# Gathering and summing the rows of the experts on chip, by matrices of zeros and ones on TensorE, in a two-block transformer kernel

## The chip, the cores and the metric

The kernel runs on one core of a Trainium2 chip (trn2), as one launch. The metric is the device time of one execution in microseconds. Before the change it is 2328.91 us, the median of three runs (2328.08 to 2332.37).

## What is computed

512 tokens of width 1024 in float32 go through two transformer blocks. The first has two kinds of attention and a mixture of experts, then a norm; the second starts with a norm of its own, a retention and a latent attention, then a feed-forward layer.

```
x = x + hybrid_mixer(rms_norm(x, attn_norm), ...)
h = rms_norm(x, ffn_norm)
x = x + hier_moe(h, w_group, b_group, w_expert, b_expert, w1, w3, w2)
x = rms_norm(x, final_norm)          # end of the first block
xn = rmsnorm(x, pre_mix_norm_2)      # start of the second block
...

def hier_moe(h, ...):
    # softmax over 8 groups, the best group; in it the best 2 of 8 experts
    gate = g_w * softmax(top_v)                # two gates per token
    expert_id = g_idx * 8 + top_i              # two of 64 experts per token
    # rows of a token go to its experts
    ys[e] = (silu(xb @ w1[e]) * (xb @ w3[e])) @ w2[e]     # 1024 -> 512 -> 1024
    out[token] += gate * ys                    # a sum of two rows per token
```

There are 1024 assignments (512 tokens, two experts each). The three matrices of one expert hold 6 MiB in float32, those of all 64 experts 384 MiB.

## The kernel before

Every engine has its own program, and semaphores tie them together; nothing is scheduled by a planner, so the order on each engine is the order of the code. SyncE (SP) issues all loads of weights, ScalarE (ACT) small loads, GpSimd (POOL) the indirect DMAs.

**Dense parts.** x (4 tiles of 128 tokens) stays in SBUF. Weights come in units of 8 KiB per partition into `raw` (three slots). ACT copies a unit to `w_hi` (`hi_until`, L622, the copy is L631) and DVE puts the rest into `w_lo` (`lo_until`, L634, the subtraction is L640); both have two slots. PE multiplies in three passes (L562 to L564) and waits for `w_lo` in `loaded`. `order` is the list of all units; those from `n_first` on belong to the second block, and `ahead` asks for the unit behind the one that is in use. `pe_to_feature` (L557) turns tokens into features by transposes; `dve_split_jobs` and `act_split_jobs` (L670, L657) take the result apart.

**Routing.** DVE makes `h2`, the normed rows (L1976), PE transposes it, the router's matmuls (L1780) give 72 logits per token, and `dve_route` (L1091) takes the best group and its two best experts. `onehot` and `both` are 0/1 rows over the 64 experts; PE sums them by `C("before")` and `C("ones")` into the rank of each assignment in its expert. DVE then makes `pos_t`, 512 times the expert plus the rank. Experts are worked in blocks of 32 rows (`BLK`); one with more than 32 assignments would get further blocks, listed behind the first 64, and `blk` holds block, expert and count. In these inputs the loop works 64 blocks.

**From lists to rows.** POOL scatters the assignment ids by `pos_t` into `slot_ids` in HBM (eight indirect DMAs, L2047), reads them back (L2051), DVE casts them (L1189), PE transposes them (L1814), and DVE writes `asg_tab` (L1194) and `tok_tab` (L1197). Then it raises `m_ready`, for which SP, PE, ACT, DVE and POOL wait. `h2` goes to `h_rows` in HBM (L2042).

**The loop over pairs of blocks** (`pe_pair`, `act_pair`, `dve_pair`, `pool_pair`; u is 0 or 1 in a pair, the last pair stands outside the loop). POOL copies a column of the table and gathers a block's rows from `h_rows` to `Xe` (L2060). PE transposes them (`rows_to_columns`, L1825, eight transposes), ACT copies them to `XTs` (L1661). `hidden(u, h)` (L1834) multiplies half of the 1024 features by half of w1 and w3: 16 matmuls, in which four column groups of PE work side by side. DVE copies the result to `Hs` (L1985), PE transposes it (L1862), ACT applies Silu (L1676), DVE multiplies by the other half (`aT`, L1987), and `down(u, h)` (L1843) multiplies by w2, 16 matmuls for both h. ACT copies that to `y_b` (L1680), and POOL scatters it to `y_rows` in HBM (L2065), a row per assignment and quarter.

**The ring.** Weights of experts lie in twelve slots of 1 MiB, six per u: four for w1 and w3, two for w2. SP loads the twelve of the first pair ahead of the routing; in the loop it reloads a slot when `w_used` says that PE has done with it (L1531). PE waits for `landed` of each.

**Behind the loop.** POOL waits for all scatters (`m_done`) and reads `y_rows` back in four DMAs (L2100). DVE adds gate times row, two per token tile (L2001), ACT squares x (L539), the root follows (`dve_rstd`, L544, L548, L550), DVE writes the normed x with the final gain (L2009), ACT squares it again for the second norm, and DVE writes `xn` (L2016), for whose four tiles PE waits in `pe_second` before the transposes hT3. Meanwhile ACT and DVE have split two units of weights, between these steps. `dve_second` (L1200) then begins with the angles of the rotations (`dve_angles`, L855) and asks for further units behind them.

PSUM's banks in the loop: bank 0 for the rows' transposes, 1 for those of the hidden rows, 2 and 3 for the hidden products of u = 0 and 1, 4 and 5 for the down products.

Of the kernel before, what the change touches and what calls it, by code (L numbers as in the profile page):

```python
# [20 lines left out]
F32 = mybir.dt.float32  # L21
# [8 lines left out]
P = 128  # L30
# [36 lines left out]
def constants():  # L67
# [41 lines left out]
    put("id2", np.concatenate([2.0 * (p + P * np.arange(NT)[None, :]) + k for k in range(2)], 1))  # L109
# [14 lines left out]
def route_constants():  # L124


    a = np.zeros((P, 128), np.float32)
# [4 lines left out]
    a[:, 97] = np.arange(P) // BLK  # L132
# [54 lines left out]
def build(nc, a, out):  # L187
    ctx = ExitStack()
    with ctx:
# [47 lines left out]
        y_b = [at(f"y_b{u}", F0 + 5120 + Q * u, [Q]) for u in range(2)]  # L237
        Xe = [at(f"Xe{u}", F0 + 28672 + D * u, [D])[0:BLK, :] for u in range(2)]
# [23 lines left out]
        h_rows = nc.dram_tensor("h_rows", (T, D), F32, kind="Internal").ap()  # L262
        y_rows = nc.dram_tensor("y_rows", (8 * T, Q), F32, kind="Internal").ap()
        c_rows = nc.dram_tensor("c_rows", (H1, T), F32, kind="Internal").ap()
        slot_ids = nc.dram_tensor("slot_ids", (NE * T, 1), I32, kind="Internal").ap()
# [169 lines left out]
        plan("ids", 2)  # L435
# [452 lines left out]
        w_used = sem("w_used")  # L888
        xt_filled, xt_out = sem("xt_filled"), sem("xt_out")
# [3 lines left out]
        gathered, scattered = [sem(f"gathered{u}") for u in range(2)], [sem(f"scattered{u}") for u in range(2)]  # L893
        idx_copied = sem("idx_copied")
        m_done, m_ready = sem("m_done"), sem("m_ready")
        pe_step, pool_step = sem("pe_step"), sem("pool_step")
        XTb, Ab = banks[0], banks[1]
        Hb, Yb = banks[2:4], banks[4:6]
# [3 lines left out]
        tok_tab = scratch[0:BLK, 0:NE * EB].bitcast(I32)  # L902
        asg_tab = scratch[:, 1024:1024 + NE * EB].bitcast(I32)
        idx_t = [scratch[0:BLK, 2048 + u:2049 + u].bitcast(I32) for u in range(2)]
        idx_a = [scratch[:, 2050 + u:2051 + u].bitcast(I32) for u in range(2)]
# [7 lines left out]
        rcst = side[:, 1696:1696 + 128]  # L913
# [4 lines left out]
        pos_t = av(2100, 8).bitcast(I32)  # L918
        id_t = av(2108, 8).bitcast(I32)
        sentinel = av(2200, 256).bitcast(I32)  # L920
        ids_raw = av(2460, 256, 8).bitcast(I32)
        ids_f = av(2720, 1024, 8)


# [166 lines left out]
        def dve_route(v, chain):  # L1091
# [53 lines left out]
            for i, job in enumerate(J["rank"]):  # L1145
                full(v, job)
                for k, junk in enumerate((masked[:, i, :], e[:, i, :])):
                    ins = v.tensor_tensor_reduce(junk, banks[job.bank][:, 0:NE], onehot[:, i, k, :], 1.0, 0.0,
                                                 ALU.mult, ALU.add, rank[:, i, k:k + 1])
                    if k:  # L1150
                        free(ins, job)
# [981 lines left out]
```

## Time and profile before

| what | value |
| --- | --- |
| median of three runs | 2328.91 us |
| the profiled execution, whole | 2332.82 us |
| its span, first to last instruction | 2331.0 us |
| mean granted TensorE clock | 0.851 |
| PE busy | 1789.6 us (77%) |
| DVE, ACT, POOL busy | 595.5, 581.9, 171.6 us |
| ring loads from SP | 384 of 1 MiB, 26.9 us from issue to landing (median) |
| HBM read, written | 510.47 MB, 12.73 MB |

A profile shows one execution. Busy time is that in which an engine worked on an instruction; "idle before" is what stood ahead of it, with the instruction or transfer that ended the wait. The profiled execution lies 3.9 us above the median. A granted clock of 1.00 is 2.4 GHz and one of 0.50 is 1.2 GHz; values between are means over a stretch. Float32 matmuls show as two instructions each.

### The profile page before, as it was taken

To read this page: it belongs to the slowest core of one execution; us is meant where nothing else is said; L and a number is where in the kernel's file an instruction comes from. 1 tells how busy PE (TensorE), PEld (TensorE's weight loads), DVE (VectorE), ACT (ScalarE), POOL (GpSimd) and SP (SyncE) were. 2 spreads that over 40 slices of the span, in tenths; PEclk is the share of its full clock that TensorE was granted. 3 is DMA by queue.
4 is the path that set the end of the run, shared out by engine and by line. 5 is a ranking of instruction groups with operands and counts; after the bars stand their busy time and mean duration, and the time that the engine had idled before them with its cause. 6 is when DMAs were issued, how large, how long until landed. Compare 5 with 4: busy or idle time off the path is not lost. (4 is left out here: it accounts for less than half of the span.)

```text
span 2331.0 us, 31203 instructions
## 1 busy us (share of the span) xinstructions
PE 1789.6 (77%) x12156; PEld 1221.0 (52%) x12156; DVE 595.5 (26%) x1085; ACT 581.9 (25%) x978; POOL 171.6 (7%) x290
## 2 busy tenths in 40 slices
PE   6998998656656666666666666379998899998988
PEld 4765787533333333333333333167745678886876
DVE  4437225400000000000000000364365342332145
ACT  3337322111111111111111111232336432221142
POOL 0000000121111111111111111000000000000000
PEclk9999999877787767677777677589989999999999
DMA  5330221669999999999999999522110222323320
GB/s 150 100 100 11 61 102 50 257 233 415 411 412 414 413 411 415 412 414 409 410 412 408 407 404 408 191 73 66 57 36 19 82 73 91 108 81 120 107 73 37
DMA packets 136626, 515.80 MB, mean 221 GB/s; under 512 B 20300, under 2 KB 67848, under 8 KB 86640
## 3 DMA queue, kind: packets, MB, share of 16 engines
q1 hardware_dynamic: 122336, 491.03, 54.3%
q0 software_dynamic: 8272, 17.09, 2.1%
q10 hardware_dynamic: 5952, 6.76, 1.0%
q8 instruction: 47, 0.77, 0.1%
q14 instruction: 19, 0.16, 0.0%
HBM read 510.47 MB, written 12.73 MB: 224 GB/s over the span
## 5 line engine op out<-in xcount | busy, mean ns | idle before, releaser
L1834 PE MATMUL bank<-ring,XTs 128*32 128x256 f32 x4096 | 362.4, 515 | 259.7 <-DMA ring<-in_w 258.7
L1834 PEld LDWEIGHTS bank<-ring,XTs 128*32 128x32 f32 x4096 | 177.9, 142 | 441.7 <-issue 415.6
L562 PE MATMUL bank<-hTh,w_hi 128*128 128x512 f32 (+1 forms) x728 | 290.2, 399 | 8.7 <-DVE w_lo L640 5.8
L640 DVE TENSOR_TENSOR w_lo<-raw,w_hi 128x2048 fp32r<-128x2048 f32 (+3 forms) x84 | 184.3, 2196 | 438.1 <-ACT w_hi L631 438.1
L563 PE MATMUL bank<-hTh,w_lo 128*128 128x512 f32 (+1 forms) x728 | 287.7, 395 | 0.0
L564 PE MATMUL bank<-hTl,w_hi 128*128 128x512 f32 (+1 forms) x728 | 287.1, 394 | 0.0
L1843 PE MATMUL bank<-ring,aT 128*32 128x256 f32 x2048 | 187.9, 522 | 94.0 <-DVE aT L1987 80.6
L1985 DVE COPY Hs<-bank 128x256 f32<-128x256 f32 x64 | 27.2, 424 | 829.8 <-PE bank L1834 829.8
L631 ACT ACTIVATE w_hi<-raw 128x2048 fp32r<-128x2048 f32 (+3 forms) x84 | 153.7, 1832 | 247.2 <-PE bank L564 239.5
L1661 ACT ACTIVATE XTs<-bank 128x256 f32<-128x256 f32 x64 | 24.5, 383 | 635.9 <-PE bank L1825 635.9
L1843 PEld LDWEIGHTS bank<-ring,aT 128*32 128x32 f32 x2048 | 74.1, 142 | 178.9 <-DVE aT L1987 96.0
L562 PEld LDWEIGHTS bank<-hTh,w_hi 128*128 128x128 f32 (+1 forms) x728 | 137.2, 188 | 49.2 <-DVE w_lo L640 12.2
L563 PEld LDWEIGHTS bank<-hTh,w_lo 128*128 128x128 f32 (+1 forms) x728 | 137.3, 189 | 31.3 <-issue 1.0
L564 PEld LDWEIGHTS bank<-hTl,w_hi 128*128 128x128 f32 (+1 forms) x728 | 137.1, 188 | 30.3 <-issue 0.2
L2065 POOL DMA_INDIRECT y_rows<-y_b,scratch x64 | 65.4, 1021 | 798.0 <-ACT y_b L1680 780.4
L562 PE MATMUL bank<-w_hi,ffh 128*128 128x512 f32 x256 | 102.2, 399 | 8.7 <-DVE w_lo L640 7.1
L564 PE MATMUL bank<-w_lo,ffh 128*128 128x512 f32 x256 | 101.6, 397 | 0.0
L562 PE MATMUL bank<-w_hi,hTh 128*128 128x512 f32 (+2 forms) x232 | 83.9, 362 | 6.3 <-DVE hTl L669 6.3
L557 PE MATMUL bank<-cst,arena 128*128 128x128 f32 x148 | 24.4, 342 | 81.6 <-DVE arena L2016 40.2
L1825 PEld LDWEIGHTS bank<-cst,Xe 32*128 32x128 f32 x512 | 61.0, 197 | 44.5 <-issue 44.5
L564 PE MATMUL bank<-w_lo,hTh 128*128 128x512 f32 (+2 forms) x232 | 83.5, 360 | 0.0
L563 PE MATMUL bank<-w_hi,hTl 128*128 128x512 f32 (+2 forms) x232 | 83.5, 360 | 0.0
(343 smaller groups left out, 2045.5 us busy)
## 6 DMA issues: line engine op xcount, KB each, us to landing
ring<-in_w SPq DMA_DIRECT2D x384, 1024.0 KB, 26.9
raw<-in_w_in SPq DMA_DIRECT2D x24, 1024.0 KB, 5.4
raw<-in_w_gate SPq DMA_DIRECT2D x11, 1024.0 KB, 5.4
raw<-in_w_up SPq DMA_DIRECT2D x11, 1024.0 KB, 5.4
raw<-in_w_down SPq DMA_DIRECT2D x11, 1024.0 KB, 4.9
raw<-in_w_out SPq DMA_DIRECT2D x4, 1024.0 KB, 5.0
arena<-y_rows POOLq DMA_DIRECT2D x4, 1024.0 KB, 8.0
raw<-in_w_o SPq DMA_DIRECT2D x4, 1024.0 KB, 4.9
```

The costliest lines, as they stand in the source:

```text
L557: mm = pe.transpose(banks[job.bank][:, P * i:P * (i + 1)], src(i, c), ident)
L562: pe.matmul(dst, left[0], right[0], start=start, stop=False)
L563: pe.matmul(dst, left[1], right[0], start=False, stop=False)
L564: return pe.matmul(dst, left[0], right[1], start=False, stop=stop)
L631: act.activation(w_hi[:, k % PARTS, 0:size], raw[:, k % RAW, 0:size], ACT.Copy).then_inc(hi_made, 1)
L640: v.tensor_tensor(w_lo[:, k % PARTS, 0:size], raw[:, k % RAW, 0:size], w_hi[:, k % PARTS, 0:size].bitcast(F32), ALU.subtract).then_inc(lo_ ...
L1661: act.activation(XTs[u][:, :, :], XTb[:, 0:DC * BLK].rearrange("p (a b) -> p a b", a=DC), ACT.Copy).then_inc(xt_out, 1)
L1825: mm = pe.transpose(XTb[:, BLK * c:BLK * (c + 1)], Xe[u][:, c:D:DC], ident[0:BLK, 0:BLK])
L1834: mm = pe.matmul(Hb[u][BLK * j:BLK * (j + 1), 0:Q], XTs[u][:, 4 * h + c, :], w[:, at_:at_ + Q], start=(h == 0 and c == 0), stop=(h == 1 an ...
L1843: mm = pe.matmul(Yb[u][BLK * j:BLK * (j + 1), 0:Q], aT[:, r, h, :], ring[6 * u + 4 + h][:, at_:at_ + Q], start=(h == 0 and r == 0), stop=( ...
L1985: v.tensor_copy(Hs[:, :], Hb[u][:, 0:Q]).then_inc(h_out, 1)
L2065: pool.indirect_dma_start(y_rows, bass.IndirectOffsetOnAxis(ap=idx_a[u].bitcast(U32), axis=0), y_b[u][:, :], None, bounds_check=last_row, ...
```

## The change

1. The lists go. No ids are scattered or read back, `h_rows`, `y_rows` and `slot_ids` are dropped. Instead DVE keeps `tab`: for every token and expert the place (rank plus one, 0 where the token is not in the expert) and the gate. `blk` holds the expert and the block's number in it.
2. Gather: POOL copies a block's columns of `tab` to `sel` and the numbers of its 32 places to `nums`; DVE compares the two (`choose`), which gives `oh`, 128 tokens x 4 tiles x 32 places of zeros and ones; PE multiplies `oh` by `h2` (`gather`, 16 matmuls, four column groups side by side), ACT copies the 128x256 result to `xe`, PE transposes it (`rows_to_columns`, now two transposes) and ACT copies that to `XTs`. For this the features of `h2` are stored in another order (`by_eighths`), and the router's weights are loaded in the same order.
3. Sum: `weigh` multiplies `oh` by the gates (`og`), PE transposes it once per pair (`gates_to_rows`), ACT copies it to `g2`. The down products of both blocks of a pair go to `y2` in four copies each. In the next pair PE multiplies `g2` by `y2` (`scatter`, four token tiles, two matmuls each), and DVE adds the result to x from PSUM (`flush`).
4. Hs, XTs and so on share fewer banks, since four are taken for the sums.
5. The norms: DVE multiplies x by the final gain (`xg`) while ACT squares x; ACT then squares `xg` without waiting for the normed x, and the second root follows from both sums. POOL writes the normed x later, beside the next steps. ACT splits its two units of the second block's weights ahead of the last copies to `y2`; DVE asks for one unit (`lo_until(v, n_first)`) before the norms.

The diff, cut to its core:

```diff
-        XTb, Ab = banks[0], banks[1]
-        Hb, Yb = banks[2:4], banks[4:6]
+        Xp, Tp = banks[0][:, 0:Q], banks[0][:, Q:2 * Q]
+        Ab, Hb, Yb = [banks[1 + k][:, 0:Q] for k in range(3)]
+        Sb = [[banks[4 + 2 * k + n] for n in range(2)] for k in range(2)]
+        Gb = Sb[1][1]
...
# dve_route
-                for k, junk in enumerate((masked[:, i, :], e[:, i, :])):
-                    ins = v.tensor_tensor_reduce(junk, banks[job.bank][:, 0:NE], onehot[:, i, k, :], 1.0, 0.0,
-                                                 ALU.mult, ALU.add, rank[:, i, k:k + 1])
...
+                free(v.scalar_tensor_tensor(by_tile[:, i, :], banks[job.bank][:, 0:NE], 1.0, both[:, i, :], ALU.add,
+                                            ALU.mult), job)
+            for k, part in enumerate((masked, e)):
+                chain(v.tensor_tensor(part, onehot[:, :, k, :], gates[:, :, k:k + 1].broadcast_to([P, NT, NE]), ALU.mult))
+            chain(v.tensor_tensor(by_tile[:, NT:2 * NT, :], masked, e, ALU.add))
...
-            v.wait_ge(S("ids_in"), 16)
...
# scalar engine
+            full(act, J["router"][-1])
+            row(gain_fin, "final_norm", D, S("w_fin"))
...
             def act_pair(i, last):
                 for u in range(2):
                     if u == 0 or not last:
+                        act.wait_ge(xe_filled, 2 * i + (u + 2))
+                        gathered_out()
                         act.wait_ge(xt_filled, 2 * i + (u + 2))
-                        rows_out(1 - u)
+                        columns_out(1 - u)
+                    if u == 1:
+                        act.wait_ge(g_filled, i + 1)
+                        act.activation(g2[:, :], Gb[:, :], ACT.Copy).then_inc(g_out, 1)
...
+                    if u and last:
+                        hi_at.limit = len(order)
+                        hi_until(act, n_first + 1)
                     act.wait_ge(w_used, 2 * STEPS * i + STEPS * (u + 1))
-                    act.wait_ge(scattered[u], 16 * i + 16)
-                    act.activation(y_b[u][:, :], Yb[u][:, 0:Q], ACT.Copy).then_inc(y_out, 1)
+                    act.wait_ge(s_filled, 4 * i + 4)
+                    for j in range(4):
+                        to = 64 * (j // 2) + BLK * u
+                        act.activation(y2[to:to + BLK, Q * (j % 2):Q * (j % 2 + 1)], Yb[BLK * j:BLK * (j + 1), :],
+                                       ACT.Copy).then_inc(y_out, 1)
...
# tensor engine
+            def gather(u):
+                for t in range(NT):
+                    for j in range(4):
+                        mm = pe.matmul(Xp[BLK * j:BLK * (j + 1), :], oh[u][:, t, :], h2[:, t, Q * j:Q * (j + 1)],
+                                       start=(t == 0), stop=(t == NT - 1))
+                mm.then_inc(xe_filled, 1)
+            def rows_to_columns():
+                for r in range(2):
+                    mm = pe.transpose(Tp[:, P * r:P * (r + 1)], xe[:, P * r:P * (r + 1)], ident)
+                mm.then_inc(xt_filled, 1)
+            def gates_to_rows():
+                for t in range(NT):
+                    mm = pe.transpose(Gb[:, P * t:P * (t + 1)], og[:, t, :, :, :].rearrange("p n u s -> p (n u s)"), ident)
+                mm.then_inc(g_filled, 1)
+            def scatter(i, t):
+                pe.wait_ge(flushed, 4 * i + (t + 5))
+                for n in range(2):
+                    rows_ = slice(2 * BLK * n, 2 * BLK * (n + 1))
+                    mm = pe.matmul(Sb[t % 2][n][:, :], g2[rows_, P * t:P * (t + 1)], y2[rows_, :], start=True, stop=True)
+                mm.then_inc(s_filled, 1)
...
             def pe_pair(i, last):
                 for u in range(2):
                     pe.wait_ge(xt_out, 2 * i + (u + 1))
...
+                    hidden(u, 0)
                     if u == 0 or not last:
-                        pe.wait_ge(gathered[1 - u], 16 * i + (16 if u == 0 else 32))
-                        rows_to_columns(1 - u)
+                        pe.wait_ge(made_oh, 2 * i + (u + 2))
+                        gather(1 - u)
+                    if u == 0:
+                        pe.wait_ge(g_out, i + 1)
+                        pe.wait_ge(y_out, 8 * i + 8)
+                        scatter(i, 0)
+                        scatter(i, 1)
...
+                    hidden(u, 1)
+                    if u == 0 or not last:
+                        pe.wait_ge(xe_out, 2 * i + (u + 2))
+                        rows_to_columns()
+                    if u == 1:
+                        pe.wait_ge(made_og, 2 * i + 2)
+                        pe.wait_ge(flushed, 4 * i + 10)
+                        gates_to_rows()
                     pe.wait_ge(h_out, 2 * i + (u + 1))
...
                         down(u, h)
+                    if u == 0:
+                        scatter(i, 2)
+                        scatter(i, 3)
...
# vector engine
+            def flush(i, t, done=None):
+                v.wait_ge(s_filled, 4 * i + (t + 1))
+                v.wait_ge(flushed, 4 * i + (t + 3))
+                for n in range(2):
+                    xs = x[:, t, 512 * n:512 * (n + 1)]
+                    ins = v.tensor_tensor(xs, xs, Sb[t % 2][n][:, :], ALU.add)
+                ins.then_inc(flushed, 1)
+            def dve_pair(i, last):
+                for u in range(2):
+                    if u == 0 or not last:
+                        choose(1 - u, 4 * i + (2 * u + 4))
+                    if u == 0:
+                        flush(i, 0)
+                        flush(i, 1)
                     v.wait_ge(w_used, 2 * STEPS * i + (STEPS * u + 2))
...
-            v.wait_ge(m_done, 1)
             lo_at.limit = len(order)
-            for i in range(NT):
-                v.wait_ge(S(f"y_back{i}"), 16)
...
-            lo_until(v, n_first + 1)
+            lo_until(v, n_first)
+            v.wait_ge(S("w_fin"), 16)
+            for t in range(NT):
+                flush(count + 1, t)
+                v.wait_ge(flushed, 4 * count + (t + 11))
+                v.sem_inc(S("x2pre"), 1)
+                v.tensor_tensor(xg(t), x[:, t, :], gain_fin, ALU.mult).then_inc(S("xg"), 1)
+            dve_rstd(v, chain, "n3", ssq, rstd, NT, D)
+            v.sem_inc(S("r3"), 1)
+            v.wait_ge(S("norm_squares"), NORMS["n4"])
+            chain(v.tensor_tensor(rstd2, rstd, rstd, ALU.mult))
+            chain(v.tensor_tensor(rstd2, rstd2, ssq2, ALU.mult))
+            v.tensor_scalar(rstd2, rstd2, 1.0 / D, EPS, ALU.mult, ALU.add).then_inc(S("norm_means"), 1)
...
# gpsimd engine
+            pool.wait_ge(S("r3"), 1)
             for i in range(NT):
-                pool.dma_start(ring_y(i), y_rows[8 * P * i:8 * P * (i + 1), :].rearrange("(p k j) n -> p k (j n)", k=2, j=D // Q))\
-                    .then_inc(S(f"y_back{i}"), 16)
+                pool.wait_ge(S("xg"), i + 1)
+                pool.tensor_scalar(x[:, i, :], xg(i), rstd[:, i:i + 1], None, ALU.mult).then_inc(S("x2"), 1)
```

## Rows read from the trace of the kernel before

**Rows 1.** The page's slices, 40 equal parts of the span, in tenths.
```profile
PEclk9999999877787767677777677589989999999999
DMA  5330221669999999999999999522110222323320
```

**Rows 2.** Windows: stretch, length, busy time and count per engine, clock, DMA share, GB/s.
```profile
700.00:1400.00 700.00, 447.80 (x4669) 230.15 (x4672) 31.64 (x89) 103.84 (x178) 104.07 (x176) 0.73 1.01 411
455.00:460.00 5.00, 4.15 (x26) 3.98 (x25) 1.89 (x17) 0.00 (x0) 0.32 (x1) 0.50 1.02 431
1452.00:1454.00 2.00, 2.00 (x25) 1.01 (x21) 0.00 (x0) 0.00 (x0) 0.00 (x0) 0.50 1.02 423
1462.00:1464.00 2.00, 1.58 (x32) 0.94 (x32) 0.29 (x1) 0.04 (x1) 0.00 (x0) 1.00 0.25 107
```

**Rows 3.** Timeline of the loop: start, duration, instruction, idle before and its releaser.
```profile
503.41 1.94 PE L1843 MATMUL bank<-ring,aT 128*32 128x256 f32 x32 [0.69 <-DVE aT L1987]
505.16 3.64 PE L1834 MATMUL bank<-ring,XTs 128*32 128x256 f32 x64
...
509.72 0.50 PE L1862 MATMUL bank<-cst,Hs 128*128 128x128 f32 x2
...
512.18 3.40 PE L1843 MATMUL bank<-ring,aT 128*32 128x256 f32 x32 [1.95 <-DVE aT L1987]
...
515.73 0.38 ACT L1680 ACTIVATE y_b<-bank 128x256 f32<-128x256 f32 x1 [3.93 <-PE bank L1843]
...
530.79 3.64 PE L1834 MATMUL bank<-ring,XTs 128*32 128x256 f32 x32 [3.13 <-DMA ring<-in_w]
...
540.22 0.42 DVE L1985 COPY Hs<-bank 128x256 f32<-128x256 f32 x1 [16.10 <-PE bank L1834]
...
1475.51 0.42 DVE L1985 COPY Hs<-bank 128x256 f32<-128x256 f32 x1 [13.14 <-PE bank L1834]
```

**Rows 4.** Timeline from the routing to the loop's first matmul.
```profile
463.75 0.14 DVE L1186 TENSOR_SCALAR small<-small 1x1 int32<-1x1 int32 x1
...
478.93 0.68 DVE L1197 TENSOR_SCALAR scratch<-scratch 32x1024 int32<-32x1024 int32 x1
480.75 0.18 POOL L2069 COPY scratch<-scratch 32x1 int32<-32x1 int32 x1 [7.69 <-issue]
...
486.54 5.98 PE L1834 MATMUL bank<-ring,XTs 128*32 128x256 f32 x64 [0.67 <-ACT XTs L1661]
```

**Rows 5.** Groups behind the loop (the last one: first block): busy us, mean ns | idle before.
```profile
L539 ACT ACTIVATE arena<-x 128x1024 f32<-128x1024 f32 x8 | 8.5, 1058 | 13.7 <-DVE x L2001 12.0 <-DVE x L2009 1.6
L2009 DVE SCALAR_TENSOR_TENSOR x<-x,small,side 128x1024 f32<-128x1024 f32 x4 | 4.9, 1280 | 0.0
...
L631 ACT ACTIVATE w_hi<-raw 128x2048 fp32r<-128x2048 f32 x2 | 3.7, 1901 | 4.1 <-POOLq L2094 4.1
L557 PE MATMUL bank<-cst,arena 128*128 128x128 f32 x13 | 3.0, 425 | 40.2 <-DVE arena L2016 40.2
...
L2016 DVE TENSOR_SCALAR arena<-x,small 128x1024 f32<-128x1024 f32 x4 | 2.7, 748 | 0.0
...
L1968 DVE TENSOR_TENSOR x<-x,bank 128x512 f32<-128x512 f32 x8 | 5.5, 686 | 21.0 <-PE bank L564 21.0
```

**Rows 6.** DMA queues from 700 to 1400 us: packets, MB, share of 16 engines.
```profile
q1 hardware_dynamic: 38718, 281.94, 98.9%
q0 software_dynamic: 4224, 5.61, 2.4%
```

**Rows 7.** Timeline of the first attention: one step's score matmuls of two heads.
```profile
174.11 1.13 PE L704 MATMUL bank<-arena 64*128 64x512 f32 x4
```

**Rows 8.** Timeline of the second block's first projection.
```profile
1526.74 0.19 PEld L562 LDWEIGHTS bank<-hTh,w_hi 128*128 128x128 f32 x1
...
1547.74 0.43 DVE L867 TENSOR_SCALAR tail<-tail 128x512 f32<-128x512 f32 x1
...
1554.56 0.80 PE L562 MATMUL bank<-hTh,w_hi 128*128 128x512 f32 x1 [5.57 <-DVE w_lo L640]
```

More of the change, by code:

```diff
@@ L1101, in dve_route @@
             gidx = rwork[:, 180:181]
-            rank, place, den = tiles(700, 2), tiles(708, 2), tiles(716, 1)
+            den = tiles(716, 1)
             masked = tiles(720, NE)
@@ L1684, in _ @@
             act_pair(count, True)
-            act.wait_ge(m_done, 1)
-            hi_at.limit = len(order)
-            hi_until(act, n_first + 1)
-            def combined(i):
+            act.wait_ge(S("w_fin"), 16)
+            for i in range(NT):
                 act.wait_ge(S("x2pre"), i + 1)
-                if i == 1:
-                    row(side[:, 0:1024], "final_norm", D, S("w_fin"))
-            act_sumsq(act, chain, "n3", lambda i: x[:, i, :], NT, arena[:, 8192:8192 + D], ssq, combined)
+                chain(act.activation(av(9216, D), x[:, i, :], ACT.Square, accum_out=ssq[:, i:i + 1]))
+            act.sem_inc(S("norm_squares"), 1)
             act.dma_start(scratch[:, 0:2048], a["decays"]).then_inc(S("w_dec"), 16)
@@ L1873, in _ @@
             pe_pair(count, True)
-            pe.wait_ge(y_out, 2 * count + 4)
+            pe.wait_ge(g_out, count + 2)
+            pe.wait_ge(y_out, 8 * count + 16)
+            for t in range(NT):
+                scatter(count + 1, t)
+            pe.wait_ge(flushed, 4 * count + 14)
             for job in J["before_moe"]:
@@ L2053, in _ @@
-            pool.wait_ge(scattered[1], 16)
+            chain(pool.memset(y2[:, :], 0.0))
+            chain(pool.memset(g2[:, :], 0.0))
+            pool.sem_inc(y_out, 8)
+            pool.sem_inc(g_out, 1)
+            pool.sem_inc(flushed, 6)
             pool.wait_ge(m_ready, 1)
             count = pool.value_load(blk[0:1, NX:NX + 1], min_val=NE // 2 - 1, max_val=NBLK // 2 - 1)
-            last_token, last_row = pool.to_reg(T - 1), pool.to_reg(8 * T - 1)
-            def gather(u):
-                pool.sem_inc(pool_step, 1)
-                pool.indirect_dma_start(Xe[u], None, h_rows, bass.IndirectOffsetOnAxis(ap=idx_t[u].bitcast(U32), axis=0),
-                                        bounds_check=last_token, oob_is_err=False).then_inc(gathered[u], 16)
@@ L2089, in _ @@
-            with pool.Fori(0, count) as i:
-                pool_pair(i, False)
-            pool_pair(count, True)
-            for u in range(2):
-                pool.wait_ge(scattered[u], 16 * count + 32)
-            pool.sem_inc(m_done, 1)
+                    expert = pool.value_load(blk[0:1, bass.ds(2 * i + (u + 2), 1)], min_val=0, max_val=NE - 1)
+                    part = pool.value_load(blk[0:1, bass.ds(2 * i + (NBLK + u + 2), 1)], min_val=0, max_val=EB)
+                    pool.wait_ge(made_og, 2 * i + (u + 1))
```

239 lines of the change are left out of this document (103 added, 136 removed).

## The prediction

> **What bounds the kernel now.** I read the page's slices first, then the windows of the expert stage, its DMA queues, and the timeline of its start, its middle and its end. The slices show one long plateau from about 490 to 1,480 us: DMA busy at nine tenths or more, PE's granted clock at 0.6 to 0.8 and so moving between its two levels (1.2 and 2.4 GHz) [rows 1]. That is the loop over 64 blocks, one per expert here (64 copies L1985 in the page). The windows confirm it: 1.01 of the DMA engines' time, 411 GB/s, PE busy 448 of 700 us, mean clock 0.73 [rows 2]. So the loop is bound by weights. The Hs copies of the fifth and the last expert stand 1475.51 - 540.22 = 935.3 us apart for 59 experts, 15.85 us each [rows 3]; the six 1 MiB loads of one are 6.29 MB, so weights arrive at 397 GB/s. Before and after the loop two chains of small steps hold everything: DVE has block table and count at 463.9, but the loop's first matmul runs at 486.5 [rows 4]; and PE waits 40.2 us between the last expert and the next block's transposes [rows 5].
>
> **Part 1, the loop's DMA.** The change removes the gathers and scatters. In 700 us they moved 5.61 MB beside 281.94 MB, and took 2.4% of the engines' time [rows 6]. Three prices follow for an expert. By bytes, weights alone at the 411 GB/s of the stage take 6.29/411 = 15.31 us. By time, 2.4% off 15.85 is 15.47. Against flat-out rates, 431 GB/s when only the first loads and the row table run, and 423 in the last microseconds of full loading [rows 2], it is 14.6 to 14.9. One row says that bytes alone understate it: from 1462 to 1464, after the last ring loads were issued, 107 GB/s and 0.25 of the engines' time remain, four engines' worth, while the other twelve are done [rows 2]. A block's rows are few (16 of 32 on the mean) and sit in its low slots, so I read this as an uneven load: every 1 MiB load waits for the engines that also carry the small transfers. I take 418 GB/s, about midway between 411 and 423 to 425, that is 15.05 us: 0.80 us less, times the 62 reloaded experts **-50 us**. The bounds are 0 (something else holds 397 GB/s) and -78 (at 431).
> The Trainium skill (DMA: Bandwidth & Descriptors, Where 436 GB/s comes from) puts the ports' ceiling at 435 GB/s and names about 358 as the HBM side's limit for one core; by the second nothing would be left to gain, and this trace, at 411 and 431, disagrees with it. By the first the loop's gain would be 86 us; no row here reaches it.
>
> **Part 2, PE in the loop.** Per pair of experts, at the clock's upper level: hidden products 2 x 3.64, down products 2 x 1.94 [rows 3]; gathers, each with half the matmuls of the hidden products and their shape, 2 x 1.82; gates_to_rows, twice the two Hs transposes of 0.50, 1.0; rows_to_columns and Hs transposes 4 x 0.50; scatters 4 x 1.13, since the attention's two heads (64x512, on the two halves of the rows, two banks, as here) take 1.13 us together [rows 7]; waits for aT 0.69 and, with a table load in it, 1.95 [rows 3]. Sum 7.3 + 3.9 + 3.6 + 1.0 + 2.0 + 4.5 + 2.6 = 24.9 us, against 30.1 of DMA. So 5 us stay hidden, if the clock is mostly up: matmuls double at the lower level (3.40 for the 32 that take 1.94) [rows 3], 19.3 us of the sum, so it fits up to 27% of them low. I price it at nothing, the cover being the weight loads; without cover it costs 0.19 us per pair and percent. Other engines have room: ACT per pair 4 copies of PSUM 256 wide, g2, 8 quarter copies for y2 of at most 0.38 each [rows 3], two Silus and two table loads of 1.28, about 9 us; DVE eight adds of 0.69 [rows 5] and small ones, about 9. The y2 copies wait for scatters 2 and 3 and ACT's next gather copy stands behind them, but PE has the next hidden product to do. The new waits of PE on flushed are behind DVE's two adds (1.4 us), which run beside hidden(0,1). POOL's two small copies replace the indexing; nothing is late on it. SP's reloads wait for the same w_used counts, so a slot of the first pair comes free a little later: +1.
>
> **Part 3, before the loop.** Removed from the path are eight scatters of ids, their return, the conversion, eight transposes and two table writes: DVE reaches L1186 at 463.75 and ends L1197 at 479.6 [rows 4]. Added on DVE are some six one-row operations at 0.14 to 0.2; rank needs four products for eight reductions, three wider ones are added: about even, m_ready at 464.5. After it: POOL as now 1.1 us to its first copy [rows 4], two copies 0.4, oh 0.4, gather at the low level 3.5, xe 0.5, transposes 0.7, XTs 0.5: 7.1, against 6.9 now. So the first hidden product moves from 486.5 to 471.6, **-15 us**. h2 is read with a stride of eight: 0 to +5 (doubling the four writes of 1.28), I take 0, for the element count is the same. The constants' load grows, but it is issued ahead of the ring loads, beside a DMA with room: 0. The final gain's 512 KiB move into the loop's first microseconds, 1.2 us of its DMA, which the same load no longer takes behind it: inside the rounding. The 2 MB of h_rows go, off the path, since the first loads are all there by 462 in any case.
>
> **Part 4, behind the loop.** Now 40.2 us. Then: ACT's two weight splits of 1.9 stand ahead of the last y2 copies and need raw tiles that land behind the last ring load, 3.5 in sum; y2 1.7; first scatter 1.9 (low level); four tiles of two adds and one 1024-wide product, 2 x 0.69 + 1.28 = 2.66 each [rows 5], 10.6; last square and root 2.5; four squares of xg 5.0 (1.06 and the accumulator read) [rows 5]; the short rstd2 chain 1.5; four scalings of 0.75 [rows 5], 3.0. Sum 29.7: **-11 us**. POOL's x2 is only needed at rv, but may stretch the scalings beside it: 0 to +2.
> One thing gets later. L640 for the second unit ran before the transposes; now lo_until stops at n_first, and the next call stands behind dve_angles, whose last operation ends at 1548.2 [rows 8]. PE's rq matmuls begin at 1526.7 and end 5.6 us ahead of 1554.6 [rows 8], 22.2 us for four jobs, so PE runs out of the first unit after 11.1, at 1537.8 of the old axis. The second w_lo ends at 1550.5; PE then works low for its first dozen matmuls (+2.5) and ends the unit at 1564.2, where today it starts the third at 1554.56 and pays the same 2.5 there [rows 8]. **+7 us**, and the ramp already there goes.
>
> Sum: -50 + 1 - 15 - 11 + 7 = -68. The profiled execution took 2332.8, the median of the three runs shown is 2328.9, 3.9 less, so 2264.8 by the first and 2261 by the second.
>
> **The rivals.** (a) Weights come no faster, or only as bytes say. For it: in the loop PE, ACT and DVE read SBUF while 431 was seen beside a nearly idle PE; against it: the four engines' tail. Part 1 gives 0 to -30: 2281 to 2311. (b) Loads reach 431 or more, Part 1 gives 78 to 86: 2225 to 2233 and up to the forecast's edge. For it, the short rows of pure loading; against, that the loop's own best stretch is 423. (c) **Slower**: PE takes over as the bound with its clock down. Place: PE inside a pair; price 31 pairs times what the pair exceeds. The other parts net -18, so it costs what it saves once a pair takes 31.7 + 18/31 = 32.3 us, that is when 7.4 of the 19.3 us, 38%, run low. For it: today the level is low for (1 - 0.73)/0.5 = 54% of the time [rows 2], and at 512.18 it was low straight after matmuls without any DMA wait, behind transposes and a table load [rows 3]; the new pair has more transposes in a row. At 54% the pair is 24.9 + 10.4 = 35.3, the loop's 31 pairs 112 us more than now, and with the -18 of the other parts 2423. Against: the low stretches of today mostly follow DMA waits, as that of 3.13 us at 530.8 [rows 3], and a PE that is behind has none, so the clock should return as load grows. The Trainium skill (TensorE: Matmul & The Clock Gate, Part 4) says that transposes do not count as PE activity for the clock; this trace agrees at 512.18, and by that rule alone (c) gains weight. (d) Within it, PE a little over DMA, 30.1 to 32 per pair, say a serial scatter: 2275 to 2320, shared with (a). (e) The change does nothing to the loop because gathers ran elsewhere: excluded, the queue row shows them.
>
> **How the numbers follow.** Forecast (2240 to 2281) 0.60; (a) with (d) 0.22; (b) 0.09; (c) 0.06; 0.03 for what I have missed, on either side. The range 2234 to 2306 holds the forecast, most of (a), and leaves out most of (b), all of (c) and the top of (a), under 0.2. A measurement of this kernel tells 0.2%, 4.7 us, from no change. Faster by more: 0.60 + 0.22 + 0.09 + 0.01 = 0.92; same 0.02, slower 0.06.
>
> **What would show it.** Right: the Hs copies 15.0 to 15.2 us apart, no share of 0.25 in the loop's last microseconds, mean clock in the loop above 0.85, first L1834 group near 472, PE's wait before hT3 near 30 us, a new wait of PE for L640 near 13 us in rq. Wrong: PE waiting for aT, flushed or y_out rather than for ring, a pair over 31.7 us, a mean clock at 0.7 or below with PE busy above nine tenths, or DVE's strided L1976 group at 2.5 us.

## The result, and the profile after

The kernel after takes **2259.07 us** (median of four runs, 2256.7 to 2259.82) against 2329.26 (four runs, 2328.08 to 2332.37): a ratio of 0.9695, 95% interval 0.9678 to 0.9712, 70 us less. The forecast was 2261. The profiled execution took 2256.7 whole, its span is 2254.9 against 2331.0, 76.1 less.

The page of the kernel after, its slices:

```profile
PEclk9999999889999999999999999799999899999999
DMA  5330121569999999999999999122110123233220
GB/s 155 103 104 11 56 94 56 220 250 422 422 422 422 422 422 422 422 422 422 422 422 422 422 422 413 62 87 60 43 49 29 58 92 102 86 111 114 94 75 38
```

In the plateau of [rows 1] the clock has gone from 6 to 8 tenths up to 9, and the loads run at 422 GB/s in slice after slice without a dip. The windows say the same of the stretch of [rows 2] (columns as there), and of the last microseconds of the loop:

```profile
700.00:1400.00 700.00, 530.50 (x6648) 277.35 (x6648) 184.97 (x426) 188.52 (x397) 15.54 (x92) 0.93 1.01 422
...
1400.00:1402.00 2.00, 1.77 (x32) 1.13 (x32) 0.00 (x0) 0.00 (x0) 0.00 (x0) 1.00 1.03 422
```

PE is busy 530 of 700 us instead of 448, and its clock is up at 0.93. The share of 0.25 at the loop's end [rows 2] is gone. The queues of 700 to 1400 us, against [rows 6]: no q0, and q1 carries 4.7% more.

```profile
q1 hardware_dynamic: 40545, 295.29, 101.3%
```

The Hs copies of the seventh and the last expert:

```profile
553.04 0.42 DVE L2065 COPY Hs<-bank 128x256 f32<-128x256 f32 x1 [0.17 <-PE bank L1858]
...
1402.22 0.42 DVE L2065 COPY Hs<-bank 128x256 f32<-128x256 f32 x1 [5.39 <-PE bank L1858]
```

That is 849.18 us for 57 experts, **14.90 us each** (6.29 MB at 422 GB/s). I count from the seventh, because the first six run ahead of the loads here, bound by PE: their copies stand 23.6 us apart per pair. In the kernel before the seventh starts at 570.45 and the last at 1475.51 [rows 3], 15.88 each:

```profile
570.45 0.42 DVE L1985 COPY Hs<-bank 128x256 f32<-128x256 f32 x1 [14.91 <-PE bank L1834]
```

What PE waited for from 460 to 1500 us (total, times, longest):

```profile
PE bank L1858 <- DMA ring<-in_w: 118.4, 54, 3.9
PE bank L1867 <- DVE aT L2071: 89.3, 64, 1.7
PE bank L558 <- DVE arena L2102: 19.4, 1, 19.4
PE bank L563 <- DVE w_lo L641: 12.6, 1, 12.6
PE bank L1849 <- ACT y L1696: 8.6, 1, 8.6
```

The loop is still bound by weights (first row). The wait for aT is a step inside every expert, hidden by the loads. The last three lie behind the loop, one after the other on the path. In front of the loop:

```profile
426.92 7.95 DVE L2024 SCALAR_TENSOR_TENSOR arena<-x,small,side 128x1024 f32<-128x1024 f32 x4 [0.26 <-DVE small L551]
...
467.19 0.14 DVE L1198 TENSOR_SCALAR small<-small 1x1 int32<-1x1 int32 x1
...
469.01 3.64 PE L1830 MATMUL bank<-arena,oh 128*32 128x256 f32 x32 [4.30 <-DVE oh L2033]
...
474.29 1.93 PE L1858 MATMUL bank<-ring,XTs 128*32 128x256 f32 x32 [0.66 <-ACT XTs L1669]
```

The first hidden product starts at 474.29 (486.54 before [rows 4]); count and table are there at 467.3, and the four strided products for h2 take 7.95 us, where L1976 took 4.87. Behind the loop:

```profile
1408.61 1.91 ACT L632 ACTIVATE w_hi<-raw 128x2048 fp32r<-128x2048 f32 x1 [5.05 <-DMA raw<-in_w_in]
...
1411.62 1.91 ACT L632 ACTIVATE w_hi<-raw 128x2048 fp32r<-128x2048 f32 x1 [1.10 <-DMA raw<-in_w_in]
1413.55 1.57 ACT L1696 ACTIVATE y<-bank 32x256 f32<-32x256 f32 x4
...
1417.46 1.28 DVE L2051 TENSOR_TENSOR x<-x,bank 128x512 f32<-128x512 f32 x2 [4.62 <-PE bank L1849]
...
1430.60 12.10 POOL L2155 TENSOR_SCALAR x<-arena,small 128x1024 f32<-128x1024 f32 x4 [69.37 <-DVEq L2091]
...
1435.28 1.02 DVE L2096 TENSOR_SCALAR small<-small 128x4 f32<-128x4 f32 x1
...
1437.41 4.40 DVE L2102 TENSOR_SCALAR arena<-arena,small 128x1024 f32<-128x1024 f32 x4
1441.87 5.73 PE L558 MATMUL bank<-cst,arena 128*128 128x128 f32 x32 [19.38 <-DVE arena L2102]
```

Put together, on the time from one mark to the next, before and after:

| from, to | before | after | difference | forecast |
| --- | --- | --- | --- | --- |
| start to first hidden product | 486.54 | 474.29 | -12.3 | -15 |
| to the last Hs copy | 988.97 | 927.93 | -61.0 | -49 |
| to the transposes of hT3 | 45.70 | 39.65 | -6.1 | -11 |
| to the first copy of rk (end of rq) | 41.51 | 48.71 | +7.2 | +7 |
| to the end | 768.28 | 764.32 | -4.0 | 0 |
| sum | 2331.0 | 2254.9 | -76.1 | -68 |

Of the last row 2.8 us are one group of eight matmuls: it met the lower clock level before (0.50 from 1700 to 1705 us) and mostly the upper one after (0.84 from 1627 to 1632). In the timeline of the kernel before:

```profile
1700.15 7.19 PE L1025 MATMUL bank<-arena,cst 4*128 4x512 f32 x8 [2.53 <-DVE arena L1257]
```

And in that of the kernel after:

```profile
1627.55 4.44 PE L1034 MATMUL bank<-arena,cst 4*128 4x512 f32 x8 [2.54 <-DVE arena L1259]
```

The change doesn't touch that code; where such a group falls between the clock's two levels moves a whole run by a few microseconds. For the other 1.2 us of the row I have no cause. This profiled execution is the fastest of the four, 2.4 us under their median.

### The profile page after: what moved, and what is told of

Same layout as the page of the kernel before. It is cut to its first block, busy times and chain, and to the rows that moved or that the text cites. A ratio compares the mean times of both kernels' runs of the same rounds, so it can differ in the third digit from the quotient of the medians.

```text
span 2254.9 us, 36572 instructions
## 1 busy us (share of the span) xinstructions
PE 1864.1 (83%) x14468; PEld 1264.4 (56%) x14468; DVE 798.6 (35%) x1526; ACT 693.5 (31%) x1266; POOL 40.8 (2%) x150
## 4 chain that ended last, share of the span: by engine, by line
PE 49%; DMA 34%; DVE 8%; ACT 4%; issue 2%; SPq 1%; ACTq 0%; DVEq 0%; POOLq 0%; POOL 0%
DMA ring<-in_w 33%; PE bank L563 12%; PE bank L564 12%; PE bank L565 12%; PE bank L1858 5%; DVE w_lo L641 2%; DMA raw<-in_w_in 2%; ACT w_hi L632 1%; PE bank L705 1%; PE bank L558 1%; PE bank L729 1%; PE bank L717 1%; SPq L1530 1%; PE bank L1830 1%; ACT arena L540 1%
## 5 line engine op out<-in xcount | busy, mean ns | idle before, releaser
L1858 PE MATMUL bank<-ring,XTs 128*32 128x256 f32 x4096 | 283.0, 422 | 119.1 <-DMA ring<-in_w 118.4
L2051 DVE TENSOR_TENSOR x<-x,bank 128x512 f32<-128x512 f32 x264 | 163.9, 683 | 473.5 <-PE bank L1849 473.5
L1858 PEld LDWEIGHTS bank<-ring,XTs 128*32 128x32 f32 x4096 | 143.2, 119 | 265.2 <-issue 213.0
L1867 PE MATMUL bank<-ring,aT 128*32 128x256 f32 x2048 | 124.0, 382 | 89.8 <-DVE aT L2071 89.3
L1696 ACT ACTIVATE y<-bank 32x256 f32<-32x256 f32 x256 | 96.0, 375 | 220.7 <-PE bank L1849 136.7
L1830 PE MATMUL bank<-arena,oh 128*32 128x256 f32 x2048 | 142.0, 422 | 8.5 <-DVE oh L2033 8.5
L1849 PE MATMUL bank<-y,g 64*128 64x512 f32 x528 | 133.0, 622 | 10.0 <-ACT y L1696 8.6
L1830 PEld LDWEIGHTS bank<-arena,oh 128*32 128x32 f32 x2048 | 79.9, 125 | 70.3 <-issue 22.8
L1666 ACT ACTIVATE xe<-bank 128x256 f32<-128x256 f32 x64 | 24.5, 383 | 278.5 <-PE bank L1830 278.5
L1849 PEld LDWEIGHTS bank<-y,g 64*128 64x128 f32 x528 | 45.8, 188 | 70.2 <-issue 66.6
## 6 DMA issues: line engine op xcount, KB each, us to landing
ring<-in_w SPq DMA_DIRECT2D x384, 1024.0 KB, 25.1
```

The source lines that it names most:

```text
L1666: act.activation(xe[:, :], Xp, ACT.Copy).then_inc(xe_out, 1)
L1696: act.activation(y2[to:to + BLK, Q * (j % 2):Q * (j % 2 + 1)], Yb[BLK * j:BLK * (j + 1), :], ACT.Copy).then_inc(y_out, 1)
L1830: mm = pe.matmul(Xp[BLK * j:BLK * (j + 1), :], oh[u][:, t, :], h2[:, t, Q * j:Q * (j + 1)], start=(t == 0), stop=(t == NT - 1))
L1849: mm = pe.matmul(Sb[t % 2][n][:, :], g2[rows_, P * t:P * (t + 1)], y2[rows_, :], start=True, stop=True)
L1858: mm = pe.matmul(Hb[BLK * j:BLK * (j + 1), :], XTs[u][:, 4 * (c % 2) + 2 * h + c // 2, :], w[:, at_:at_ + Q], start=(h == 0 and c == 0), s ...
L1867: mm = pe.matmul(Yb[BLK * j:BLK * (j + 1), :], aT[:, r, h, :], ring[6 * u + 4 + h][:, at_:at_ + Q], start=(h == 0 and r == 0), stop=(h == ...
```

## What the loop gained from

Two theories of the 0.98 us per expert, four kernels first. U: the row transfers load few of the sixteen engines and every weight load waits for those. B: they cost only their bytes, and the rest came from the new order of the work. Three kernels take transfers out of the kernel before. In `gather` and in `scatter`:

```diff
-                pool.indirect_dma_start(Xe[u], None, h_rows, ...).then_inc(gathered[u], 16)
+                pool.sem_inc(gathered[u], 16)
...
-                pool.indirect_dma_start(y_rows, ..., y_b[u][:, :], ...).then_inc(scattered[u], 16)
+                pool.sem_inc(kept[u], 16)
```

> Kernel before, without the loop's gathers (all but the first two) and without its scatters; semaphores are raised in their place. Left out: every expert works on the rows of the first two, and the rows that come back after the loop are read from w1 instead. Theory U (the row transfers load few DMA engines, and each weight load waits for these): the whole gain of the loop is theirs, so the Hs copies stand 14.9 us apart as in the kernel after (15.88 in the kernel before, 7th to last copy) and the time is 2329 - 61 = 2268, give or take 5. Theory B (they cost only their bytes, 0.127 MB of an expert at 411 GB/s, 0.31 us; the rest of the gain came from the new order of PE's and ACT's work): 15.57 us and 2310.

> Kernel before, without the loop's gathers (all but the first two); scatters stay. Left out: the experts work on the rows of the first two. Theory U: a gather's 16 rows of 4 KB lie on the fewest engines, so most of the 0.98 us is its: Hs copies 15.2 apart, time near 2285. Rival W (writes to HBM between the reads are what costs, so the scatter carries most): 15.7 and 2317. Theory B: 15.73 and 2319.

> Kernel before, without the loop's scatters; gathers stay. Left out: the experts' results; the rows after the loop are read from w1. Theory U: Hs copies 15.6 apart, time near 2312. Rival W (writes): 15.1 and 2280. Theory B: 15.73 and 2319.

Measured (each once, beside 2332.26 for the kernel before on the same chip):

| kernel | Hs copies apart | time |
| --- | --- | --- |
| without both | 14.91 | 2260.22 |
| without gathers | 15.21 | 2282.88 |
| without scatters | 15.57 | 2307.68 |

Without both, the old loop streams exactly as fast as the new one: **the whole gain of the loop comes from the row transfers**, none from the order of PE's work. B falls. The prices are 0.30 us for a scatter and 0.66 for a gather, and they add up to the 0.97 between 15.88 and 14.91, so rival W, writes, falls too: a gather carries two thirds for the same 64 KB. The seventh and the last Hs copy of the kernel without both, and its window:

```profile
562.56 0.42 DVE L1986 COPY Hs<-bank 128x256 f32<-128x256 f32 x1 [13.21 <-PE bank L1835]
...
1412.49 0.42 DVE L1986 COPY Hs<-bank 128x256 f32<-128x256 f32 x1 [12.68 <-PE bank L1835]
...
700.00:1400.00 700.00, 449.83 (x4954) 241.94 (x4958) 33.44 (x94) 107.46 (x186) 16.59 (x93) 0.79 1.01 422
```

Windows of the one without scatters, the last two from the loop's end:

```profile
700.00:1400.00 700.00, 449.99 (x4770) 234.14 (x4762) 32.04 (x90) 103.02 (x178) 58.38 (x134) 0.75 1.01 412
...
1446.00:1448.00 2.00, 0.93 (x20) 0.28 (x11) 0.00 (x0) 0.38 (x1) 0.00 (x0) 1.00 0.46 193
1454.00:1456.00 2.00, 1.71 (x32) 1.13 (x32) 0.00 (x0) 0.00 (x0) 0.00 (x0) 1.00 0.31 125
```

The tail of a few busy engines is there with gathers alone. With scatters alone it is there too, less deep; a window of the kernel without gathers:

```profile
1426.00:1428.00 2.00, 0.49 (x8) 0.00 (x0) 0.00 (x0) 0.00 (x0) 0.00 (x0) 0.50 0.49 207
```

The other way round, plain transfers of the same bytes added to the kernel after, in `pool_pair`:

```diff
+                    pool.wait_ge(wrote[u], 16 * i + 16)
+                    pool.sem_inc(side_step, 1)
+                    pool.dma_start(side_y[64 * u:64 * u + 64, :], cst[0:64, 0:Q]).then_inc(wrote[u], 16)
+                    pool.wait_ge(fetched[u], 16 * i + 16)
+                    pool.sem_inc(side_step, 1)
+                    pool.dma_start(side_x[32 * u:32 * u + 16, :], a["x"][0, 16 * u:16 * u + 16, :]).then_inc(fetched[u], 16)
```

> Kernel after, with two plain transfers added per expert, issued by POOL: 64 rows of 1 KB written to HBM and 16 rows of 4 KB read from it, the same bytes and rows as the kernel before's scatter and gather, but without indices. Theory U: plain transfers are cut over all 16 engines, so they cost little more than their bytes, Hs copies 15.2 apart (14.90 in the kernel after) and 2259 + 19 = 2278. Rival S (any small transfer between the large ones costs the same, whatever its form): 15.9 and 2320.

Measured: 15.64 us per expert, 2307.89 us. Theory U as I had put it, that plain transfers are spread and so cheap, is wrong by 30 us. The write has little part in it (0.14 us of the 0.74, as the first of the next runs shows). That is half of the 0.30 of a scatter of the same bytes; no run varies where the rows of a write lie, so what sets the price of a write stays open. So the next three ask what in the read costs. All leave out the write; they differ only in where the same 64 KB land.

```diff
-  side_x[32 * u:32 * u + 16, :]        <- 16 rows of 4 KB             # a_read16
+  side_x[u:P:8, :]                     <- 16 rows of 4 KB             # a_read16s
+  side_x[:, P * u:P * (u + 1)]         <- 128 pieces of 512 B         # a_read128
```

> Kernel after, with one plain read per expert, issued by POOL: 16 rows of 4 KB into 16 neighbouring partitions (the read of a_direct without its write). a_direct cost 0.74 us per expert, the kernel before's gather 0.66, its scatter 0.30. Theory P (what costs is where the rows land: 16 neighbouring partitions, on whose way the weight loads' packets queue): most of a_direct's price is here, 0.6 us per expert, Hs copies 15.5 apart and 2259 + 37 = 2296. Rival V (the mix of writes and reads is what costs): 0.2 us, 15.1 and 2271.

> The same read of 16 rows of 4 KB, but into every eighth partition of the 128. Theory P: only its bytes are left, 0.15 us per expert, 15.05 and 2268. Rival R (rows of 4 KB cost, or any read on a second queue, wherever it lands): as a_read16, 15.5 and 2296.

> The same 64 KB read as 128 pieces of 512 B into all 128 partitions. Theory P: its bytes, 15.05 and 2268. Rival R, if the row's size is what costs: 15.05 as well; if any read on a second queue costs: 15.5 and 2296.

| 64 KB read per expert into | Hs copies apart | over 14.90 | time |
| --- | --- | --- | --- |
| 16 neighbouring partitions | 15.50 | 0.60 | 2302.23 |
| every eighth partition | 15.25 | 0.35 | 2279.38 |
| all 128 | 15.15 | 0.25 | 2269.94 |

Queue (POOL's) and bytes are the same in the three. The first two have the same 16 rows of 4 KB too, so between them only the landing place changes the price, from 43 us to 20 over the kernel after. The third, 11 us, also has shorter pieces. Theory P holds, with one miss: every eighth partition costs more than its bytes. The prices follow nearly if the landing is shared by sixteen ways of equal rate and the fullest way sets the pace (estimates from the windows): one way carries 422/16 = 26.4 GB/s; 64 KB on four of them is 16.4 KB each, 0.62 us; on eight 0.31; on all sixteen 0.16. Measured 0.60, 0.35, 0.25; the last has 0.09 more than this, which no run explains. The 107 GB/s at a share of 0.25 in [rows 2] are the rate of four such ways. Whether the ways are the DMA engines or places behind them, no run tells.
The Trainium skill (SBUF — State Buffer, Door 1: The DMA port swizzle (why `[64,N]` ≈ `[32,N]`)) gives the map: sixteen ports with eight partitions each, by which the lowest 16 partitions lie on four ports and every eighth partition on eight. These runs agree with both, to 0.02 and 0.04 us of the estimates.
One sign stays open. I had read the tail at 0.25 as the mark of the uneven load, but a_read16 has the price without the tail; in its last full stretch all engines are busy:

```profile
1440.00:1442.00 2.00, 0.00 (x0) 0.00 (x0) 0.00 (x0) 0.00 (x0) 0.00 (x0) 1.00 1.04 434
```

So the lag that adds up over the loop belongs to the indirect form, while the price is nearly that of a plain read (0.66 against 0.60). Why, no run here tells.

## Whether PE is near to being the bound

Every gather on PE done three times over, for the rivals (c) and (d):

```diff
-                for t in range(NT):
+                for t in [*range(NT)] * 3:
                     for j in range(4):
                         mm = pe.matmul(Xp[BLK * j:BLK * (j + 1), :], oh[u][:, t, :], ...)
```

> Kernel after, with every gather product on PE done three times over (same values, same place). While both first experts' weights are there, a pair takes 23.6 us, bound by PE; two more gathers of 1.94 us in each half make 31.4, against 29.8 of weight loads. If PE is hidden up to the loads' time and its clock holds: pairs 31.4 apart, 1.6 over, 31 of them, 2259 + 50 + 8 for the first two pairs = 2317, PE busy nearly all the time and clock above 0.95. Rival C (the clock falls with more small operations in a row, the slower case of the forecast): at half of the matmuls low, a pair of 45 us and 2730. Rival H (PE has more room than the sum says): 2262.

Measured: 2304.94 us; the copies stand 30.53 us apart per pair. Its window:

```profile
700.00:1400.00 700.00, 628.69 (x9392) 362.18 (x9388) 177.18 (x409) 185.03 (x386) 15.41 (x90) 0.99 1.00 410
```

One gather in its timeline:

```profile
547.76 5.39 PE L1830 MATMUL bank<-arena,oh 128*32 128x256 f32 x96
```

PE is the bound here (a ring load lands 9.3 us after its issue instead of 25.1, since SP now waits for slots). Three gathers in a row take 5.39 us, 1.73 for each further one, and 23.6 + 4 x 1.73 = 30.5: the sum over PE's instructions holds to a tenth of a microsecond once a gather is put at 1.73 instead of 1.94. Rival C falls: with more of the same small matmuls, and as many transposes, the clock is 0.99. In the kernel after it is 0.93, where PE waits for loads.

## The two ends of the loop

**h2 without the stride.** DVE writes h2 as before, PE reads it with the stride of eight.

```diff
-                v.scalar_tensor_tensor(h2[:, i, :].rearrange("q (c p) -> q c p", c=DC), by_eighths(x[:, i, :]), ...
+                v.scalar_tensor_tensor(h2[:, i, :], x[:, i, :], rstd[:, i:i + 1], row_gain, ALU.mult, ...
...
-            pe_to_feature(pe, J["hT2"], lambda i, c: h2[:, i, P * c:P * (c + 1)])
+            pe_to_feature(pe, J["hT2"], lambda i, c: h2[:, i, c:D:DC])
...
-   oh[u][:, t, :], h2[:, t, Q * j:Q * (j + 1)],
+   oh[u][:, t, :], by_eighths(h2[:, t, :])[:, 2 * j:2 * j + 2, :],
```

> Kernel after, with h2 written in the order of x (DVE's four products read no stride) and the stride of eight put on PE instead, into the reads of the transposes of hT2 and of the gathers. The four products took 4.87 us in the kernel before and 7.95 in the kernel after. Theory H: 3.1 us less in front of the loop, the gathers as quick as before (1.94 us at the upper level): 2256. Rival P (PE reads every eighth element slower, so the gathers take longer; hidden in the loop up to 29.8 us per pair, but not the first one): 2258 to 2262.

Measured: 2257.87 us (2254.38 to 2259.78), ratio 0.9691 (0.9676 to 0.9706): no different from the kernel after. The time from the first h2 product to the first hidden product is 44.4 us instead of 47.4, just the 3 us. But half of each theory is true; the gather doubles, at a clock of 1.00:

```profile
520.03 3.87 PE L1830 MATMUL bank<-arena,oh 128*32 128x256 f32 x32
```

A pair then takes 27.5 us of PE instead of 23.6. That is under 29.8 and I had called it hidden, but in the first pairs PE is the bound. The clock has a part as well: it is 0.83 from 480 to 490 us, 1.00 in the kernel after, and the first down products take 3.62 us instead of 1.93:

```profile
484.96 3.62 PE L1868 MATMUL bank<-ring,aT 128*32 128x256 f32 x32 [1.70 <-DVE aT L2072]
```

Slots come free later, and from 480 to 500 us the loads move 352 GB/s instead of 410, 1.16 MB or 2.8 us of loading that nothing gives back. The gain of 3.0 is paid back within the first 20 us of the loop.

**w_lo of the second unit early again.**

```diff
             lo_until(v, n_first)
+            lo_until(v, n_first + 1)
```

> Kernel after, but DVE makes w_lo of the second unit right behind the first, as the kernel before did, 1413.5 to 1415.8, ahead of its first add at 1417.5. Theory L: PE's wait of 12.6 us in rq goes and the small one of the third unit (5.6 in the kernel before) comes back; together 7.2 us less, 2252. Rival K (the clock: the kernel after gained 3.4 us further on because eight matmuls at L1034 met the upper level, and that goes again): 2255. Rival N (the order of the splits is not what holds rq): 2259.

Measured: 2253.09 us (2252.67 to 2254.38), ratio 0.9675 (0.966 to 0.969). PE's wait for w_lo goes from 12.6 to 5.5 us, the one of the kernel before [rows 8]. Theory L holds for the wait. Rival K has its part too: in this profiled execution the eight matmuls of L1034 take 7.19 us again, not 4.44, and it is 3.6 us shorter than the profiled one of the kernel after (2253.09 and 2256.7); by the medians the gain is 6.0.

**The copies of y2 first.** ACT's two w_hi splits go behind the last copies, both w_lo splits behind the first norm's root:

```diff
-                    if u and last:
-                        hi_at.limit = len(order)
-                        hi_until(act, n_first + 1)
...
             act_pair(count, True)
+            hi_at.limit = len(order)
+            hi_until(act, n_first + 1)
...
-            lo_at.limit = len(order)
-            lo_until(v, n_first)
...
             v.sem_inc(S("r3"), 1)
+            lo_at.limit = len(order)
+            lo_until(v, n_first + 1)
```

> Kernel after, with the last quarter copies of y2 on ACT ahead of the two w_hi splits (in the kernel after they stand behind them and run at 1413.55 instead of 1406.8), and both w_lo splits on DVE behind the root of the first norm, in its wait of 4.5 us. Theory T: the last scatter, the adds and everything up to hT3 come 6.7 us earlier, and PE's wait of 12.6 us in rq goes as in a_lo: 2259 - 6.7 - 7.2 = 2245. Rival D (the end waits for raw tiles or for DVE instead, since two splits of 2.29 stand in a gap of 4.5): 2249 to 2252.

Measured: **2244.02 us** (2243.36 to 2244.6), ratio 0.9635 (0.962 to 0.965), 15 us below the kernel after. Its timeline:

```profile
1406.97 1.94 PE L1866 MATMUL bank<-ring,aT 128*32 128x256 f32 x32 [0.95 <-DVE aT L2070]
1408.96 1.57 ACT L1693 ACTIVATE y<-bank 32x256 f32<-32x256 f32 x4 [2.56 <-PE bank L1866]
1410.56 1.91 ACT L632 ACTIVATE w_hi<-raw 128x2048 fp32r<-128x2048 f32 x1
...
1425.04 4.50 DVE L641 TENSOR_TENSOR w_lo<-raw,w_hi 128x2048 fp32r<-128x2048 f32 x2
...
1436.39 5.46 PE L558 MATMUL bank<-cst,arena 128*128 128x128 f32 x32 [18.74 <-DVE arena L2100]
```

y2 is copied at once when PE is done, the splits fill ACT's idle time until the first square, and both w_lo fit into DVE's wait for the squares. From the start of the last down products to hT3 it is 29.4 us instead of 37.8, and PE's wait for w_lo in rq is 5.7 us instead of 12.6: 8.4 and 6.9, together the 15.

**Both together.**

> a_tail and a_h2 together. Their parts stand one behind the other on the path, so the gains add up: 2245 - 3 = 2242. If one of them only moves the wait, 2246 to 2252.

Measured: 2245.11 us (2240.44 to 2247.69), ratio 0.9633 (0.962 to 0.9646). The stride on PE adds nothing here either; the simpler kernel above is the best of the study.

## Why the prediction was right, by its steps

**Part 1** named the right cause, and mis-sized it. The term was 0.80 us per expert for 418 GB/s; measured are 0.98 and 422, 61 us instead of 50. That bytes alone (15.31) and mean time (15.47) understate it is shown: without the transfers the old loop runs at 14.91. What failed is "about midway between 411 and 423": the row nearest to a loop without small transfers was the 423 of [rows 2], full loading inside the loop, and the kernel runs at that, steadily. The reading of an uneven load stands in part: for a read the price hangs on where the rows land, with plain reads as well; the tail from which it was read comes only with indirect transfers. Rival (a), bytes only, is excluded by the kernel without both. Rival (b), 431 and more, is reached by no window of 700 us; the highest is 422.

**Part 2.** PE's pair was put at 24.9 us at the upper level; the first pairs, bound by PE, take 23.6. The gathers held (1.93 and 1.94 us of busy time, 1.75 and 1.87 from their start to the next group's, said 1.82). Too dear were the scatters, where two tiles take 1.99 us, so all four 4.0 instead of 4.5, and the transposes with those of the gates, 2.4 instead of 3.0; the small rest lies in the overlap of neighbouring groups. Priced at nothing, rightly: the kernel without the row transfers but with the old PE work is as fast in the loop. Rival (c) had its weight from a clock that was low for half of the time; it said itself that those stretches follow DMA waits, and that is what decided. Its other reason, "the new pair has more transposes in a row", was a misreading of the code: a pair had 20 transposes, ten in a row per expert, and has 12 now, eight in a row at most. So the Trainium skill's rule on transposes (TensorE: Matmul & The Clock Gate, Part 4), cited there, gave (c) no weight, and the clocks of 0.93 and 0.99 here do not test it. The sum also took the lower level as doubling a matmul's time; the first gather, at 0.50, takes 3.64 us against 1.94, 1.9 times.

**Part 3** said -15, measured -12.3. The step that failed is "h2 is read with a stride of eight: I take 0, for the element count is the same": four products took 7.95 instead of 4.87 us, +3.1, inside the bound of 5. Count and table come at 467.3 instead of 464.5, and the first half of this kernel ran 2.0 us ahead (h2 starts at 426.9 instead of 428.9; by chance, for in other runs here it starts between 426.8 and 429.2 with either code, once at 433.6), so the one-row operations and the table's products cost about 1.7 us more than "about even". From the table to the first hidden product it is 7.0 us, said 7.1.
The Trainium skill (Advanced Engine Details and Errata, Memory Cachelines) says that accesses that leave a 16-byte line each time pay a penalty; here one value lies 32 bytes from the next, and both DVE (1.28 to 2.04 us) and PE (1.94 to 3.87) paid it. It would have given the h2 term its sign.

**Part 4** said 40.2 to 29.7; measured are 35.2 from the end of the last down product (1406.7) to hT3. Of its terms flush and products (10.4 for 10.6), root (2.3 for 2.5) and squares (4.7 for 5.0) hold. Three were too small. ACT's splits in front of y2 cost 6.9 us instead of 3.5, since both stood waiting for raw tiles, which land at 1408.6 and 1411.6. The rstd2 chain took 2.5 instead of 1.5: a 128x4 operation on DVE that takes 0.16 elsewhere took 1.02, and L2099 0.60, while POOL wrote x2. The four scalings took 4.4 instead of 3.0, beside POOL as well (the forecast had 0 to +2). The **+7** of w_lo was right: PE's wait of 12.6 us was said to be about 13, and the end of rq comes 7.2 later.

The sum was -68 and the profiled executions show -76.1: 12 us too little for the loop, 7.9 too much for its two ends and rq, and 4.0 further on that no step had, 2.8 of them the clock's. So part of the closeness of the total is luck: the misses of the loop and of its ends cancel in large part, and the profiled execution before lay 3.6 us above its median, the one after 2.4 below, so that by the medians the gain is 70. Of the signs that were to show it right, the tail that is gone, the clock above 0.85 and the wait for w_lo came as said; the Hs copies (14.90, said 15.0 to 15.2), the first product (474.3, said 472) and the time before hT3 (35.2, said 30) did not.

## To carry to other kernels

This loop, bound by large loads, pays for a small read not by its bytes but by where it lands: 64 KB cost 0.16 us by bytes, and 0.60 when 16 neighbouring partitions took them. For small writes no such rule is shown. Before pricing such a change, look for the loop's own best full window, not for the mean between it and the present rate. And behind the end of such a loop, order each engine's first operations by who waits: what waits for a load belongs behind what is ready, which was worth 15 us here.

## What the hardware showed that was not expected

- Small reads beside a full stream of 1 MiB loads: +0.60, +0.35, +0.25 us for the same 64 KB into 16 neighbouring, every eighth, and all partitions.
- A moving operand in float32 read with a stride of 32 bytes halves PE: 32 matmuls of 256 columns in 3.87 instead of 1.94 us, both at a clock of 1.00. DVE's product goes from 1.28 to 2.04 us.
- Beside POOL's scalings of 128x1024 (2.84 us each, median) DVE's four scalings take 1.16 us (median) instead of 0.75, and one small DVE operation takes 1.02 instead of 0.16, while the two ahead of it stay at 0.16. Beside the two w_lo splits of the kernel with the copies first it is the other way round: DVE's stay at 2.25 us each, and POOL's first scaling takes 7.11 us. That POOL is the cause is read from the overlap; no run leaves POOL's work out.
- The loop's granted clock was 0.73 where PE waited longest for loads, 0.93 with the added products, and 0.99 where PE was the bound.
